# Attention's products of probabilities and values, made in two column tiles of the array

## What is computed

```
s = q @ k.T * scale + bias        # per head, 128 queries at a time, 128 or 256 keys
p = softmax(s)                    # unnormalised in the kernel: exp(s - max)
o = p @ v                         # v is 64 wide per head
```

## Time and profile before

| | |
|---|---|
| median of 3 runs | 1623.07 us (1622.53 to 1623.72) |
| profiled execution, its own time | 1622.75 us |
| its span | 1620.9 us |
| TensorE busy | 1589.0 us, 98% |
| weight loads busy | 1366.0 us, 84% |
| VectorE, ScalarE, GpSimd busy | 951.8, 802.7, 167.6 us |
| HBM traffic | 269.60 MB, mean 166 GB/s |
| longest parts of the chain that ended last | L1437, L1438, L1439 with 20% each; L1577 2%, L1694 1% |

### The profile page before, as it was taken

The page is one execution under the profiler, slowest core; times in us unless marked ns, Lnnn a source line. Parts: engine busy times, 40 slices in busy tenths (PEclk is TensorE's granted clock), DMA queues, the critical chain, the costliest instruction groups (busy, mean ns, idle before and its releaser), DMA issues.

```text
span 1620.9 us, 22861 instructions
## 1 busy us (share of the span) xinstructions
PE 1589.0 (98%) x8768; PEld 1366.0 (84%) x8768; DVE 951.8 (59%) x1454; ACT 802.7 (50%) x1358; POOL 167.6 (10%) x187
## 2 busy tenths in 40 slices
PE   9999999999999999999999999999999999999998
PEld 7888899888888888888889988888888878879886
DVE  5555475444765555555456544666554678676875
ACT  6444464445364444544355454454443556453653
POOL 1000022211200000000021222130000301010010
PEclk9999999999999999999999999999999999999999
DMA  7666455444555555655546443446665453245521
GB/s 254 202 204 211 142 183 190 132 142 125 172 174 192 183 187 166 201 187 182 192 141 204 148 141 117 144 155 215 205 213 192 147 184 125 66 156 165 176 85 53
DMA packets 76718, 269.60 MB, mean 166 GB/s; under 512 B 8512, under 2 KB 9792, under 8 KB 76608
## 3 DMA queue, kind: packets, MB, share of 16 engines
q1 hardware_dynamic: 76320, 267.35, 50.7%
q10 hardware_dynamic: 288, 0.79, 0.1%
HBM read 267.06 MB, written 1.05 MB: 165 GB/s over the span
## 4 chain that ended last, share of the span: by engine, by line
PE 73%; DVE 4%; ACT 4%; issue 2%; POOL 1%; DMA 0%; POOLq 0%; DVEq 0%; ACTq 0%
PE bank L1437 20%; PE bank L1439 20%; PE bank L1438 20%; PE bank L1443 4%; PE bank L1562 2%; PE bank L1577 2%; DVE wlo L2285 1%; PE bank L1694 1%; ACT hh L1975 1%; DVE cv L2282 1%; ACT wk L2207 1%; PE bank L1504 1%; PE bank L1500 1%; PE bank L1496 1%; ACT whi L1972 0%
## 5 line engine op out<-in xcount | busy, mean ns | idle before, releaser
L2285 DVE TENSOR_TENSOR wlo<-raw,whi 128x1024 fp32r<-128x1024 f32 (+5 forms) x472 | 565.1, 1205 | 404.2 <-ACT whi L1972 368.8
L1972 ACT ACTIVATE whi<-raw 128x1024 fp32r<-128x1024 f32 (+4 forms) x500 | 508.9, 1029 | 417.1 <-PE bank L1439 391.3
L1437 PE MATMUL bank<-whi,hh 128*128 128x512 f32 (+3 forms) x1120 | 434.2, 388 | 0.0
L1439 PE MATMUL bank<-whi,hl 128*128 128x512 f32 (+3 forms) x1120 | 425.1, 380 | 0.0
L1438 PE MATMUL bank<-wlo,hh 128*128 128x512 f32 (+3 forms) x1120 | 424.6, 379 | 0.0
L1439 PEld LDWEIGHTS bank<-whi,hl 128*128 128x128 f32 x1120 | 210.4, 188 | 38.4
L1438 PEld LDWEIGHTS bank<-wlo,hh 128*128 128x128 f32 x1120 | 210.8, 188 | 35.9
L1437 PEld LDWEIGHTS bank<-whi,hh 128*128 128x128 f32 x1120 | 210.7, 188 | 35.8
L1437 PE MATMUL bank<-hh,whi 128*128 128x256 f32 x480 | 142.4, 297 | 0.0
L1437 PE MATMUL bank<-whi,gh 128*128 128x512 f32 x352 | 139.3, 396 | 0.0
L1439 PE MATMUL bank<-whi,gl 128*128 128x512 f32 x352 | 137.9, 392 | 0.0
(11 more groups left out here) (326 smaller groups left out, 1880.4 us busy)
## 6 DMA issues: line engine op xcount, KB each, us to landing
raw<-W SPq DMA_DIRECT2D x463, 512.0 KB, 3.4
raw<-W SPq DMA_DIRECT2D x26, 384.0 KB, 3.7
raw<-W SPq DMA_DIRECT2D x8, 416.0 KB, 3.1
tab<-tab SPq DMA_DIRECT2D x6, 384.0 KB, 4.0
raw<-W SPq DMA_DIRECT2D x4, 426.0 KB, 3.1
raw<-W SPq DMA_DIRECT2D x6, 192.0 KB, 2.6
x<-x_in SPq DMA_DIRECT2D x2, 512.0 KB, 6.8
tab<-gains SPq DMA_DIRECT2D x2, 512.0 KB, 4.3
```

What stands on the lines that cost most here:

```text
L1437: e.matmul(dst, ah, bh, start=start, stop=False)
L1439: return e.matmul(dst, al, bh, start=False, stop=stop)
L1972: return e.activation(dst, src, ACT.Copy)
L2285: return e.tensor_tensor(dst, src, hi.bitcast(F), ALU.subtract)
```

## The change

Each product of `m1_values` and `m2_values` becomes two: queries 0 to 63 of the block, written to partitions 0 to 63 of the bank, and queries 64 to 127, written to partitions 64 to 127. Of the stationary operand each takes 64 of the 128 columns; the moving operand is the same. The built program gives them array tiles of 128 x 64 at column 0 and at column 64, where before there was one of 128 x 128. 264 products become 528; waits and signals stay as they are.

```diff
@@ m1_values
         for k in range(u["n"]):
-            i = e.matmul(dst, pt[:, tok(k)], vs[k], start=k == 0, stop=k == u["n"] - 1)
+            for z in range(2):
+                half = slice(64 * z, 64 * z + 64)
+                i = e.matmul(dst[half], pt[:, k * 128 + 64 * z:k * 128 + 64 * z + 64], vs[k], start=k == 0,
+                             stop=k == u["n"] - 1)
@@ m2_values
-                i = e.matmul(bank[:, u["col"][z]:u["col"][z] + 64], pt[:, tok(z * n + k)], v, start=k == 0,
-                             stop=k == n - 1)
+                for m in range(2):
+                    at = (z * n + k) * 128 + 64 * m
+                    i = e.matmul(bank[64 * m:64 * m + 64, u["col"][z]:u["col"][z] + 64], pt[:, at:at + 64], v,
+                                 start=k == 0, stop=k == n - 1)
```

## The result

The changed kernel takes 1629.85 us (median of 6 runs, 1628.33 to 1632.3), the one before 1622.96 (6 runs): a ratio of 1.0045 with an interval of 1.0034 to 1.0055. It is slower by 6.9 us; 7.2 were forecast.

What follows compares the result with a forecast made beforehand. TensorE's sequence was taken as the path, with values passes bound by their 128-column weight load. Switches 37.4 less gain 29.6, corrections -0.8 and +0.2, gave +7.2 us, so 1630.0 us; forecast range 1626 to 1637.

Steps and rivals of the forecast that it cites:

- TensorE's sequence is the path in mixer 1: First mixer's attention: TensorE busy 158.3 of 160 us, without slack, so nearly all the loss, 7.0 us, falls there.
- The pass is bound by its load: Values products: each of 528 passes costs 0.112 us for its 128-column weight load, not its stream; 59.1 us of path.
- Two tiles at once: Values products: both 64-column halves run together, 0.056 us for a pair of passes instead of 0.112, gaining 29.6 us.
- The pair of switches, 0.36 us: Around each of 104 values units: going into tiles and back out costs 0.36 us, 37.4 us in all.
- Corrections: Mixer 2: four units behind tiled lines save about 0.2 us each, -0.8; two 8-pass units ending in GpSimd waits, +0.2.
- Rival A: Values units: instruction issue or the two loads allow no second tile, losing the 29.6 us gain; about 1659 us, chance 0.09.
- Rival B: Unit edges: no drain between 128 and two times 64 columns; 18 us faster, 1605; chance 0.09 including up to break-even.
- Rival C: TensorE's 8.2 us of waits for ScalarE's wk tiles absorb at most half the added time; 1626 us, chance 0.08.

Runs made afterwards that it cites:

- one-half run: The changed kernel with only queries 0 to 63 of each block multiplied, queries 64 to 127 left out: 1627.03 us, 1.0031 of the kernel before.
- four tiles: The changed kernel with four column tiles of 32 columns in place of two of 64: 1625.40 us, 1.0023 of the kernel before.
- mixer 1 alone: The changed kernel with column tiles in the first mixer only, the second mixer's products full width again: 1628.57 us, 1.0036 of the kernel before.
- extra crossing: The changed kernel with the middle product of each of the 16 dilated units at full width: 1634.62 us, 1.0077 of the kernel before.

## Why the prediction was right

- **TensorE's sequence is the path in mixer 1**: 7.0 us were forecast there, 6.6 were found, the sum of the units' differences, and all of it is still there where mixer 2 begins.
- **The pass is bound by its load**: right. With half the columns a load is recorded with 138 ns, 54 less than the 192 of 128 columns, and the pitch of a pass goes from 0.112 us to 0.058 for its two halves together.
- **Two tiles at once**: right, and the one-half run shows it by itself. The term was 0.056 us for a pair of passes, measured 0.058, and a pass gained 0.053 where 0.056 was forecast: 528 x 0.003 = 1.6 us less gain.
- **The pair of switches, 0.36 us**: 0.34 by the line through the units, 104 x 0.02 = 2.1 us less cost. The two errors nearly cancel, -2.1 + 1.6 = -0.5, and that is luck; it is part of why the sum came out as close as it did.
- **Corrections**: the four units behind a tiled line have -0.065 and -0.28 us where their kind has +0.13 and -0.08, so 0.2 each as forecast. The two units that end in a wait for GpSimd are 0.10 and 0.08 us longer than before, where 0 was forecast and their kind gains 0.08: what they wait for is late itself by then. The error is 0.2 us.
- **The clock** is in no term, though the earlier trace rows has 0.98 for mixer 2. With the units' differences alone mixer 2 would be 0.6 us longer, and 0.6 were found; but the changed kernel's trace has one more stretch at half clock, worth up to 1.6 us, and two idle times of TensorE, 0.6 and 0.5 us, are gone. That these even out is luck. The forecast is well borne out in mixer 1 alone, where the clock is full in both.
- **Rival A** (no second tile, or issue): falls with the one-half run and, in full, with four tiles. I gave it 0.09; the four loads within 0.05 us of the earlier trace rows were worth more than that.
- **Rival B** (no drain between 128 and 64 columns): falls. The first tiled load stands 0.30 us behind the transpose's, whatever the tile's width: 0.31 for 64 and for 32 columns. From matmul to matmul it is 0.20 us, 268.39 to 268.59 above, where 0.11 is the pitch. The Trainium skill's rule that a change of mode drains TensorE (TensorEngine Tiling (Array Packing), Key Properties) agrees with this 0.20 us.
- **Rival C** (covered by waits): the waits for wk went from 8.2 to 7.8 us, and to 7.0 or 7.1 in the traces of mixer 1 alone, one half and extra crossing. It took about 1 us of 7 at most.
- The Trainium skill (TensorEngine Tiling (Array Packing), Instruction Overhead) warns against tiling what is small already. As a price this does not hold here: with four tiles, 48 matmuls of 64 columns started in 0.81 us, 17 ns each. That is less than the prediction's estimate of 25 ns from the 60 cycles given there.

## What to carry to other kernels

Column tiles pay by the run of tiled work between two switches, not by the product: here a visit costs 0.34 us and returns 0.053 us for each pass, so it takes seven passes to break even. Before a product is tiled, count the visits and see whether they can be merged; then run the new order at full width too, since the order has a price of its own that the tiles can hide. Look at the granted clock of each stretch before a few us are put down to the code. Where a load of half the array ties with the stream, narrower tiles are a little better still, by 0.02 to 0.04 us a unit here.

## What was not expected of the hardware

- Matmuls of different column tiles overtake each other. With all passes of one tile ahead of the other's in the program, the second tile started with about three passes of the first yet to begin, and a unit of 4 passes took 0.39 us in either order.
- With four column tiles TensorE starts eight instructions every 0.056 us, 7 ns each, in a unit of 96 instructions.
- Entering tiles of 15, 32 and 64 columns costs the same: 0.20 to 0.21 us between matmuls where 0.11 to 0.12 is the pitch. The whole pair of switches is 0.34 us a unit with 64 columns and 0.33 with 32.
- TensorE's granted clock fell to half in mixer 2 for one to four short stretches in every trace, also behind work in which TensorE was busy throughout, but with products of 32 moving columns. Each costs up to 1.6 us (two in a row 3.2), as much as a fourth of the change's whole effect.
